# Where five products of the input projection stand in the opening of a decoder step on one core

## What is computed

```python
c_q, c_kv, k_r, r_q, r_k, r_v, r_g = jnp.split(h @ w_in, in_split_points(), axis=-1)
...
ret = head_norm(ro).reshape(b, l, RET_HEADS * RET_DV) * jax.nn.silu(r_g)
return jnp.concatenate([mla, ret], axis=-1) @ w_out
...
q = (hb @ w_q).reshape(PEER_BLOCK, PEER_HEADS, 2, PEER_KEY_DIM // 2)
sc = jnp.einsum('thpd,hpnd->thpn', q, sub_keys).astype(jnp.float32)
s1, i1 = lax.top_k(sc[:, :, 0], PEER_TOPK)
...
act = jax.nn.gelu(jnp.einsum('thkd,td->thk', u_tab[e], hb), approximate=False)
return jnp.einsum('thk,thkd->td', gate * act, v_tab[e])
```

## Time and profile before

| | us |
|---|---|
| median of 3 runs | 3414.5 |
| lowest, highest | 3405.62, 3426.62 |
| the profiled execution, its own time | 3422.03 |
| span of its core | 3420.2 |
| TensorE busy | 2932.2 (86%) |
| VectorE busy | 2321.0 (68%) |

### The profile page before, as it was taken

One profiled execution on the slowest core, in us unless ns is written; L12 is line 12 of the kernel. 1 busy time (PEld: TensorE's weight loads), 2 busy tenths in 40 slices (PEclk: granted clock), 3 DMA queues, 4 the chain that ended last, 5 costly groups with the idle time before them and its releaser, 6 DMA issues.

```text
span 3420.2 us, 32473 instructions
## 1 busy us (share of the span) xinstructions
PE 2932.2 (86%) x9486; PEld 1512.5 (44%) x9486; DVE 2321.0 (68%) x5531; ACT 1544.6 (45%) x4211; POOL 1317.1 (39%) x1097
## 2 busy tenths in 40 slices
PE   7989899987889897988899888988897898877787
PEld 6755545543445444544444334533453344433222
DVE  1278648785687658774879578856875576766854
ACT  2147334554356334643466345634563454433343
POOL 0023334443344434343445344444443433433432
PEclk8999999998999999999999999999998998999899
DMA  4289999999999999999999999999999989799998
GB/s 179 90 331 371 379 361 413 378 409 421 394 404 386 421 422 412 384 401 422 406 397 415 422 421 422 406 421 416 392 374 408 421 335 326 301 357 394 364 422 347
DMA packets 237353, 1294.92 MB, mean 379 GB/s; under 512 B 45636, under 2 KB 70116, under 8 KB 94454
## 3 DMA queue, kind: packets, MB, share of 16 engines
q0 software_dynamic: 156672, 1140.92, 82.2%
q1 hardware_dynamic: 80502, 151.92, 11.8%
HBM read 1275.74 MB, written 16.44 MB: 378 GB/s over the span
## 4 chain that ended last, share of the span: by engine, by line
PE 46%; DMA 24%; DVE 22%; ACT 4%; issue 3%; SPq 1%; POOL 0%; DVEq 0%; ACTq 0%; POOLq 0%
PE PS L1076 21%; DVE R L1722 9%; DMA R<-in_t_uv,idx 8%; PE PS L759 7%; DMA wring<-in_w_query 6%; DMA wring<-in_w_out 6%; DMA R<-in_t_uv,idxS 3%; PE PS L998 3%; PE PS L1025 3%; PE PS L725 2%; PE PS L840 2%; PE PS L839 2%; DVE SC L1685 2%; DVE SC L1682 2%; DVE ef L1687 2%
## 5 line engine op out<-in xcount | busy, mean ns | idle before, releaser
L690 POOL DMA_INDIRECT R<-in_t_uv,idx x1024 | 1252.5, 1223 | 1981.5 <-PE PS L1076 1365.8
L1076 PE MATMUL PS<-R,diag 128*128 128x512 f32 x3616 | 1778.7, 630 | 227.3 <-ACT diag L1351 183.6
L1722 DVE CUSTOM_DVE_ANT_0 R<-R,hb 128x1024 f32<-128x1024 f32 x1088 | 1315.8, 1221 | 617.8 <-DMA R<-in_t_uv,idx 536.6
L1076 PEld LDWEIGHTS PS<-R,diag 128*128 128x128 f32 x3616 | 684.1, 200 | 1091.0 <-issue 647.8
L1342 ACT ACTIVATE acts<-dots 128x1 f32<-128x1 f32 x1088 | 216.8, 199 | 1126.5 <-DVE dots L1722 1119.0
L1351 ACT ACTIVATE diag<-ident,wv 128x128 f32<-128x128 f32 x840 | 337.7, 402 | 114.4 <-PE PS L1076 88.2
L759 PE MATMUL PS<-R 128*128 128x256 f32 (+1 forms) x1280 | 290.9, 383 | 33.2 <-ACT stg L1119 23.8
L1344 ACT ACTIVATE wv<-gate,acts 128x1 f32<-128x1 f32 x1024 | 302.0, 295 | 33.2
L759 PEld LDWEIGHTS PS<-R 128*128 128x128 f32 x1280 | 242.7, 196 | 98.4 <-issue 68.1
L1733 DVE SCALAR_TENSOR_TENSOR xb<-R,wv,xb 128x1024 f32<-128x1024 f32 x184 | 236.1, 1283 | 12.4 <-ACT wv L1344 12.4
L998 PE MATMUL PS<-wring,T 128*128 128x512 f32 x256 | 146.1, 700 | 69.1 <-DMA wring<-in_w_out 68.9
(11 more groups left out here) (242 smaller groups left out, 2394.0 us busy)
## 6 DMA issues: line engine op xcount, KB each, us to landing
wring<-in_w_out SPq DMA_DIRECT2D x64, 512.0 KB
wring<-in_w_query SPq DMA_DIRECT2D x64, 512.0 KB
R<-in_t_win SPq DMA_DIRECT2D x27, 1024.0 KB, 18.3
R<-in_t_uv,idx POOLq DMA_INDIRECT x1024
pr<-prd SPq DMA_DIRECT2D x8, 976.0 KB
prd<-stg SPq DMA_DIRECT2D x54, 128.0 KB
xb<-in_x_prompt SPq DMA_DIRECT2D x8, 512.0 KB, 8.0
R<-in_w_out SPq DMA_DIRECT2D x8, 512.0 KB, 5.3
```

The lines of the kernel that those rows point to most:

```text
L690: e.indirect_dma_start(dst, None, table, bass.IndirectOffsetOnAxis(ap=index, axis=0)).then_inc(S[s], c.count(name, s, 16))
L1076: m = mm(bank(n), diag[:, NTH[s] % DR, :], pair(s)[:, D + 512 * n:D + 512 * n + 512], start=begins, stop=s == last_slot(t), skip_group_che ...
L1722: e.tensor_tensor_reduce(u, u, hb[:, tile_of(g) % 2, :], 1.0, 0.0, ALU.mult, ALU.add, dots[:, g % NW:g % NW + 1]).then_inc(dve_done, c.cou ...
```

## The change

```diff
@@ -133,10 +133,10 @@
     it = stage("items", 0)
     first = stage("prep", 0) + it[0:2] + stage("prep", 1) + it[2:4]
     first += stage("kv", 0) + stage("kv", 1) + stage("q", 1) + mixed(stage("att", 1), stage("prep", 2) + it[4:17])
-    first += stage("meta", 0) + mixed(stage("ret", 1), it[17:21])
-    first += tail(1)[0:10] + it[21:22] + tail(1)[10:]
-    first += stage("lda", 2) + mixed(top(1, 0), it[22:26] + stage("quart", 1))
-    spread(it[26:], 0, 4)
+    first += stage("meta", 0) + mixed(stage("ret", 1), it[17:19])
+    first += tail(1)[0:10] + it[19:20] + tail(1)[10:]
+    first += stage("lda", 2) + mixed(top(1, 0), it[20:25] + stage("quart", 1))
+    spread(it[25:], 0, 3)
     spread(stage("quart", 2) + stage("quart", 3), 3, 9)
     spread(stage("kv", 2) + stage("q", 2), 9, 17)
     for piece in range(1, 4):
```

## The result

The changed kernel took 3425.84 us (median of 20 runs, 3413.48 to 3435.3), the kernel before 3417.36 in 20 runs beside it. The ratio is 1.0029, with a 95% interval of 1.0018 to 1.0040: 9.9 us longer, at least 6 and at most 14 (the two medians lie 8.5 apart). It is the side that was forecast, within the 1%, but about twice the 5.0 us of the sum.

A forecast was written before the change was run, and what follows sets the result against it. From the sort on, TensorE's work up to quarter 3, then gather 7, dot 7 and everything in turn order after it, sets the end. -2.35 - 1.35 + 1.74 + 6.96 = +5.0 us, giving 3419.5 us; range 3403 to 3434.

The forecast's parts named there:

- (a): Retention of tile 1: with item 18 gone from ahead of them, inner products start when turned keys are copied; -2.35 us.
- (b): Retention of tile 1: with item 19's copy gone, the root's table load starts right behind the sums; -1.35 us.
- (c): Loads of w_out ahead of the output projection: now issued behind item 18, costing 0 to 0.6 us; taken as 0.
- (d): Around the transposes of hb: TensorE idles some 2.4 us ahead, so the clock falls for one stretch; +1.74 us.
- (e): Output projection to sort: item 19 replaces item 21, no change; first gather 2.0 us earlier, fifth item beside sort costs nothing.
- (f): From the sort's start to slot 0: two more items on TensorE, no idle time to take them; +6.96 us.
- (g): Gathers 6 and 7: transfers hide none of the 6.96 us; dot 6 about as before, dot 7 5.5 us behind gather 7.
- rival 2: Behind the start of the retention's end: the clock does not fall at (d), total +3.3 us; chance not in the text.
- rival 3: First slots: transfers bound them, so only the first gather's start counts; -2.0 or -3.7 us; chance 0.15.
- Rival 5: Output projection, line 998: the clock stays low throughout, doubling 14.00 us; total +17.3 us, 3431.8; chance 0.08.

The follow-up runs named there:

- e4: Changed kernel with the copies of items 28 and 29 in two free places of stg, so that they wait for no store; ratio 1.0022 against the kernel before.
- e11: The changed kernel run again unaltered, beside the kernel before on the same chip; ratio 1.0021, 7.2 us longer than before.
- e6: Changed kernel plus five unused matmuls filling TensorE's two waits around the transposes of the turned keys; ratio 1.0016 against the kernel before.
- e7: e2 plus the five filler matmuls of e6; ratio 0.9971 against the kernel before, 9.9 us shorter.
- e2: Changed kernel with items 24 and 27 cut to one matmul of eight (result wrong); ratio 1.0016 against the kernel before, 5.5 us longer.
- e8: Changed kernel with the shelves and query quarter order of e5, without filler; ratio 1.0010 against the kernel before.
- e1: Kernel before with the matmuls of items 24 and 27 done twice, nothing changed ahead of the sort; ratio 1.0021, 7.2 us longer.
- e5: Kernel before with the shelves of e4, query quarter 2 in turns 0 to 2, quarter 3's projection ending turn 2, its rest in turns 4 to 8; ratio 0.9988.
- e9: Kernel before with item 18 cut in three around the turned keys' transposes and behind the output products, item 19's copy behind the root; ratio 1.0001.
- e3: Kernel before with query quarters 2 and 3 in turns 0 to 5 in place of 3 to 8; ratio 0.9985, 5.1 us shorter.
- e10: e9 with the shelves and query quarter order of e5; ratio 0.9975 against the kernel before, 8.5 us shorter, 3408.0 us.

## Why the prediction came out as it did

The side, the range and the main cost were right: forecast +5.0 us, measured +9.9 (6.2 to 13.7) and +7.2 (2.7 to 11.6). The size was half to two thirds of it. By its steps:

(a), (b): **right in mechanism, and paid only when the clock holds.** In e4 and e11 the inner products follow ScalarE's copy with a wait of 1.11 us behind the transposes (0.25 in e6 and e7, where the filler takes up the rest), which is worth 2.3 us, as (a) has it. (b) is worth 2.0 and not 1.35: it put the table load of the root behind the sums, but the load follows the squares and does not wait for them. Together that is 4.3 us for 3.7. In the changed kernel, e2 and e8 the gain is lost whole.

(c): **right for a held clock, missed for a fallen one.** No wait in e4, e6, e7 and e11. In the changed kernel, e2 and e8, 2.78 to 2.83 us, outside the bound of 0.6, because the end of item 18, which releases the loads, had gone from 133.8 to 139.8 in the changed kernel. The bound was made with item 18 at the full clock. The projection starts 3.6 us behind the first load where it waits for it, which is under the 4.6 that (c) counted on.

(d): **the step that failed.** TensorE idles 1.8 us ahead of the transposes of `hb` and not 2.4 (e4, e6, e7, e11), mostly because (b) gains more. It cost the forecast 1.7 us in e11 and nothing in the other three, where the clock held. But the same figure, short wait, transposes, wait of 1.11 for ScalarE, now also stands one stage ahead, at 122 to 125, made by the very removal of item 18 in (a). The prediction read the 1.31 us there as evidence that the clock stays (rival 2), though in that row item 18 followed the transposes at once. With the fall there the new front is 1.0 to 1.5 us slower than the old one at the first gather, instead of 2.0 faster: a miss of 3 to 3.5 us in those executions. (d) was priced at 1.74, for a low stretch of 3.4 us; this one lasted some 13, from 125 to 138, though TensorE was busy for 11.89 of twelve. Why so long, and why the clock holds in some executions, no run shows.

The Trainium skill, page "TensorE: Matmul & The Clock Gate", section "What's actually happening", calls the ramp under one per cent of a typical kernel's span. To leave it out of the sum would have given +3.3, further off than +5.0. The same passage says of the start of a kernel that the number of slow matmuls differs between runs of one kernel. Here, in the middle of a kernel, the traces show the like: the clock fell ahead of the inner products in the changed kernel and held there in e11, which is the same kernel. The loss is still far under one per cent of the span, but much larger than the 1.74. Counted from the transposes of the turned keys, the first gather of the changed kernel comes 5.7 us later than that of e4: 4.4 by the slowed work up to the transposes of `hb`, 1.7 by the wait behind them (2.78 for 1.11), since the loads on SP's queue hang on the slowed item 18, and 0.3 back in line 998.

(e), (f): **right in the main.** The first sort took as long as before with the fifth item beside it: 19.0 us from the scores of quarter 0 to the first gather in both. The 6.96 us of TensorE's work are 7.0 in the changed rows, +7.2 in time in e1, and 6.7 at gather 7 between e5 and e8. Gather 5's wait for item 25 was overlooked. **One sentence of (f) failed as well**: that the copies of items 24 to 28 wait for stores long issued. The copy of item 28 takes the shelf of item 24, whose store is now issued among the first gathers. The 128 KB stores issued between 197 and 215 landed after 10.7 us (median), those of 118 to 160 in the kernel before after 1.7:

```profile
prd<-R SPq DMA_DIRECT2D x4, 128.0 KB, 10.7
```

That is the 1.5 us more at slot 0 in the changed kernel and in e6 (1.6 in e11), and gone in e4.

(g): **right for gather 7**: dot 7 came 5.5 us behind it, as before, and rival 3 is refuted by e1. Dot 6 was not "about as before": gather 6 went out 13.2 us later, and only a shorter landing (5.8 us for 9.0 from gather to dot) brought dot 6 to 10.1 late. That the lag of dot 7 stays to the end is not shown. Against the profile of before, the changed kernel is 13.2 us behind at dot 7, 18.5 at dot 895 and 13.3 at the last dot; e1 is 13.2 behind at dot 7, 2.3 at dot 255 and 5.4 at the last; between dots 7 and 255 the difference moved by anything from +2.2 (e9) to -11.0 (e1).

Summed over what was seen: the front, at the first gather, +1.0 to +1.5 in three of five cases, -3.3 (e4) and -3.8 (e11, of which 1.4 is an earlier start of the stretch) in two, -0.7 as a mean; items +7.0; store +1.5. That is about 8. Clock losses behind the sort (3.3 in the changed kernel, 1.6 in e4) make it 9 to 11, but some kernels with the old order lose there too, so perhaps not all of it is the change's. Measured was 7 to 10. Since each of these terms is read from single executions, that the sum fits is no proof of its parts. Rival 5 (a clock that stays low through line 998) did not occur; a long low stretch did, one stage ahead. Rival 2's condition, no fall in (d), held in e4, e6 and e7; its +3.3 lies under the 6.2 of the first interval and inside that of e11.

**What stays open.** How e3 gains 5 us in time (and e5 perhaps 4) while dot 7 is not sooner in their profiles; one profile each with an unlucky quarter 0 can't tell. Also e7's 9.9, more than its 3.9 at the first gather: its profile is 2.8 ahead at dot 7 and still 2.2 at dot 767. And what decides in one execution whether the clock falls.

## What to carry to other kernels

Moving work out of a chain frees the chain only if that work was not also keeping TensorE's clock up. List the idle pieces that remain around each short group of matmuls, and price a fall at everything that hangs on the slowed work, releases of DMA included. Work moved to where TensorE has no free stretch costs its full length (7.2 us in e1 for 7.0), and moves the stores and copies tied to it into busier transfers. The gain did not need the move: fill the two waits with pieces of the item (e9), and put what releases the next gathers ahead of what does not need to be first (e10). That ends where the DMA engines are full: 10 us from gather 7 to dot 7 in e5 and e10 for 5.5.

## What was not expected of the hardware

- The clock took either of two ways through the same short waits (1.30 and 1.11 us around 1.09 of transposes): it stayed at 1.00 in e4 and e11, and went to 0.50 for over ten microseconds in the changed kernel, e2 and e8. e11 and the changed kernel are the same program. The difference at the first gather is 4 to 5 us, half of the whole effect or more.
- A small store of 128 KB took 1.7 us to land in a quiet stretch (median of five) and 10.7 us among gathers (median of four), in a stretch in which the queues took 97.6% of the 16 engines' time.
- The table load of the root did not wait for the root's input: it started at 136.08, and the sums ended at 136.73.
- Single executions differ far from the change: from dot 896 to dot 1023 they took between 399 us (e9) and 420 us (e5), 416 in the kernel before, though all kernels have the same orders there. The span of one profile says nothing about 10 us. The time to dot 7 tells what became of the opening, and only the runs together tell the time.
